# Second block's attention in a fused two-block kernel: hand-shakes by block, another order of normalising, the output projection's first two tiles together, and four of eight key copies behind the index loop

## What is computed

```python
q_lat = einsum('bshn,hnc->bshc', q_nope, w_uk)             # 8 sparse heads; the kernel turns w_uk onto the keys instead
logits = einsum('bqhd,bsd->bhqs', q_idx, k_idx)             # the index: 8 index heads
index  = einsum('bhqs,bqh->bqs', relu(logits), w_idx)       # masked causally
sel    = top_k(index, 128)                                  # keys that a query keeps
p      = softmax((q_lat . c_kv + q_rope . k_rope) * scale over sel)      # per sparse head
o_a    = (p @ c_kv) @ w_uv                                  # 8 sparse heads, 64 wide
o_b    = dilated_attention(q_b, k_b, v_b)                   # 8 dilated heads, 64 wide, a bias table in place of masks
x      = x + concat(o_a, o_b) @ w_out                       # layer "out2"
```

## Time and profile before

| | us |
|---|---|
| median of three runs (lowest, highest) | 1631.54 (1627.67, 1635.12) |
| the profiled execution | 1633.2 |
| its span | 1631.4 |
| TensorE busy | 1590.2 (97%) |
| VectorE, ScalarE, GpSimd busy | 877.9, 730.2, 599.9 |
| mean granted TensorE clock | 0.994 |

### The profile page before, as it was taken

One profiled execution on the slowest core, in us unless ns is written; L12 is line 12 of the kernel. 1 busy time (PEld: TensorE's weight loads), 2 busy tenths in 40 slices (PEclk: granted clock), 3 DMA queues, 4 the chain that ended last, 5 costly groups with the idle time before them and its releaser, 6 DMA issues.

```text
span 1631.4 us, 20643 instructions
## 1 busy us (share of the span) xinstructions
PE 1590.2 (97%) x7742; PEld 1296.7 (79%) x7742; DVE 877.9 (54%) x1117; ACT 730.2 (45%) x871; POOL 599.9 (37%) x254
## 2 busy tenths in 40 slices
PE   9999999999999899999999999889999999999997
PEld 7898887688887788888898687557878888888886
DVE  6254111781565799989875698442533642232314
ACT  5355132344244688887863422774243322221221
POOL 1421454043442133222225555554323344344441
PEclk9999999999999999999999999999999999999998
DMA  5321243222225999999964336002411222232221
GB/s 199 123 72 52 78 142 116 78 78 103 81 105 200 393 421 405 389 393 392 389 247 143 103 104 169 29 1 78 155 52 52 104 90 93 101 103 90 92 102 52
DMA packets 49617, 251.52 MB, mean 154 GB/s; under 512 B 9936, under 2 KB 12752, under 8 KB 23312
## 3 DMA queue, kind: packets, MB, share of 16 engines
q1 hardware_dynamic: 43200, 237.85, 40.0%
q0 software_dynamic: 5184, 8.40, 1.4%
q10 hardware_dynamic: 1168, 4.39, 0.7%
HBM read 235.00 MB, written 16.78 MB: 154 GB/s over the span
## 4 chain that ended last, share of the span: by engine, by line
PE 74%; issue 12%; DVE 6%; POOL 3%; ACT 2%; DMA 2%; PEld 0%; SPq 0%; ACTq 0%; DVEq 0%; POOLq 0%; PEldq 0%
PE psum L232 21%; PE psum L234 21%; PE psum L233 21%; POOL w_lo L148 3%; DVE kept_bias L2173 1%; PE psum L2320 1%; DVE top L2172 1%; PE psum L2355 1%; PE psum L2343 1%; PE psum L2600 1%; DMA moe_w<-in_w_moe 1%; PE psum L1310 1%; PE psum L710 1%; ACT w_hi L142 1%; PE psum L729 1%
## 5 line engine op out<-in xcount | busy, mean ns | idle before, releaser
L148 POOL TENSOR_TENSOR w_lo<-raw,w_hi 128x2048 fp32r<-128x2048 f32 x91 | 418.9, 4604 | 666.5 <-ACT w_hi L142 631.6
L142 ACT ACTIVATE w_hi<-raw 128x2048 fp32r<-128x2048 f32 x95 | 181.5, 1911 | 326.9 <-PE psum L234 326.8
L232 PE MATMUL psum<-x_hi,w_hi 128*128 128x512 f32 (+1 forms) x816 | 316.3, 388 | 2.4 <-ACT k_sparse L2108 1.7
L233 PE MATMUL psum<-x_lo,w_hi 128*128 128x512 f32 (+1 forms) x816 | 314.1, 385 | 0.0
L234 PE MATMUL psum<-x_hi,w_lo 128*128 128x512 f32 (+1 forms) x816 | 314.1, 385 | 0.0
L1328 DVE TENSOR_TENSOR moe_lo<-moe_w,moe_hi 128x2048 fp32r<-128x2048 f32 x100 | 228.0, 2291 | 32.7 <-ACT moe_hi L1318 31.6
L1318 ACT ACTIVATE moe_hi<-moe_w 128x2048 fp32r<-128x2048 f32 x100 | 191.2, 1915 | 28.5 <-PE psum L234 16.9
L232 PEld LDWEIGHTS psum<-x_hi,w_hi 128*128 128x128 f32 x816 | 153.3, 188 | 34.7 <-ACT k_sparse L2108 2.5
L233 PEld LDWEIGHTS psum<-x_lo,w_hi 128*128 128x128 f32 x816 | 153.3, 188 | 31.2 <-issue 0.7
L234 PEld LDWEIGHTS psum<-x_hi,w_lo 128*128 128x128 f32 x816 | 153.3, 188 | 30.7
L232 PE MATMUL psum<-y_hi,w_hi 128*128 128x512 f32 x352 | 138.0, 392 | 0.3 <-issue 0.3
(11 more groups left out here) (389 smaller groups left out, 2854.7 us busy)
## 6 DMA issues: line engine op xcount, KB each, us to landing
raw<-in_w_dense SPq DMA_DIRECT2D x95, 1024.0 KB, 4.8
moe_w<-in_w_moe_ahead SPq DMA_DIRECT2D x54, 1024.0 KB, 14.2
moe_w<-in_w_moe SPq DMA_DIRECT2D x48, 1024.0 KB, 14.9
yrow<-expert_rows SPq DMA_DIRECT2D x8, 512.0 KB, 7.2
res<-in_x SPq DMA_DIRECT2D x4, 512.0 KB, 6.6
decay<-in_decay SPq DMA_DIRECT2D x8, 256.0 KB, 5.1
hn_rows<-hn_tok ACTq DMA_DIRECT2D x4, 512.0 KB, 8.3
out<-res SPq DMA_DIRECT2D x4, 512.0 KB, 2.7
```

Of the source, the lines that this page charges most:

```text
L142: act.activation(w_hi[c % RING][:, :], raw[c % RING][:, :], ACT.Copy).then_inc(hi_ready, 1)
L148: pool.tensor_tensor(w_lo[c % RING][:, :], raw[c % RING][:, :], w_hi[c % RING][:, :].bitcast(F32), ALU.subtract).then_inc(lo_ready, 1)
L232: pe.matmul(out, lh, rh, start=first, stop=False, **more)
L233: pe.matmul(out, lh, rl, start=False, stop=False, **more)
```

## The change

1. *Index loop.* The latent keys are made after turns 3, 8, 13, 18, in banks 3, 0, 1, 2, each with its own wait for the bank. Only the first four copies stay in the loop (after turns 5, 7, 10, 12); the other four come behind it on ScalarE. q_rope waits for four copies, q_b for eight.
2. *Hand-shakes by block.* VectorE signals each of the three rest blocks, ScalarE waits for each, and TensorE signals the 384 block by itself (`s_mid`). The rest blocks get places of their own: 384 in bank 2, 256 and 128 in bank 3. S(1) waits for the v_b tiles bank by bank and not for all of them at once.
3. *Order on VectorE.* normalise(k+1) stands between softmax(k+2, 0) and softmax(k+2, 1).
4. *ScalarE's start.* The copies of the latent values are mixed with the exponentials of head 1, and the split of the second out2 chunk moves from before the head loop to its turn 4.
5. *out2.* Its first two tiles are built together, kt by kt, and the last T and V stand ahead of kt 2, 3 and 4.

```diff
-                for m in range(per):
+                if together and b == 0 and i == 0:
+                    steps = [(m, kt) for kt in range(kts) for m in range(per)]
+                else:
+                    steps = [(m, kt) for m in range(per) for kt in range(kts)]
+                for m, kt in steps:
...
-    LATENT_AT = (4, 9, 14, 19)
-    LATENT_READ_AT = tuple(u + i for u in LATENT_AT for i in (2, 3))
+    LATENT_AT = (3, 8, 13, 18)
+    LATENT_READ_AT = (5, 7, 10, 12)
+    LATENT_BANK = (3, 0, 1, 2)
...
+                latent_key(LATENT_READ_AT.index(u))
+        for h in range(HEADS // 2, HEADS):
+            latent_key(h)
         dense_act(act, "q_rope")
...
         def latent_keys(p):
-            pe.matmul(psum[:, p, :], w_uk[:, 2 * p:2 * p + 2, :].rearrange("p h c -> p (h c)"), c_kv[:, :],
+            pe.wait_ge(bank_free, FIRST_TILE["q_rope"] + p + 1)
+            pe.matmul(psum[:, LATENT_BANK[p], :], w_uk[:, 2 * p:2 * p + 2, :].rearrange("p h c -> p (h c)"), c_kv[:, :],
                       start=True, stop=True).then_inc(ql_done, 1)
...
-        pe.wait_ge(ql_read, HEADS)
         for name in ("q_rope", "q_b", "k_b"):
+            if name != "k_b":
+                pe.wait_ge(ql_read, HEADS // 2 if name == "q_rope" else HEADS)
             dense_pe(pe, name, x_hi, x_lo)
...
-    rest_z = flat[:, 1024:1024 + SPAN - S]
+    rest_z = {2: flat[:, 1024:1024 + 3 * P], 1: flat[:, 1536:1536 + 2 * P], 0: flat[:, 1792:1792 + P]}
...
-                    if h >= 2 and qt == TB - 2:
-                        pe.wait_ge(rest_read, COUNTED + h)
+                    out = rest_z[qt]
+                    if h >= 2 and qt:
+                        pe.wait_ge(rest_read, COUNTED + 3 * (h - 1) + (1 if qt == TB - 2 else 3))
+                if h == 1 and qt:
+                    pe.wait_ge(bank_free, FIRST_TILE["out2"] - 2 + 2 * (TB - 1 - qt))
+                if h == 2 and qt == TB - 1:
+                    pe.wait_ge(bank_free, FIRST_TILE["out2"] + 4)
...
-        pe.wait_ge(bank_free, FIRST_TILE["out2"] + 4)
...
-        dense_pe(pe, "out2", y_hi, y_lo, norm=Parts(av_low, COUNTED),
-                 step_hooks={4: lambda: [transposes(A_HEADS - 2), values(last - 1)],
-                             5: lambda: [transposes(A_HEADS - 1), values(last)]})
+        dense_pe(pe, "out2", y_hi, y_lo, norm=Parts(av_low, COUNTED), together=True,
+                 step_hooks={2: lambda: transposes(A_HEADS - 2),
+                             3: lambda: [values(last - 1), transposes(A_HEADS - 1)],
+                             4: lambda: values(last)})
...
         softmax(0, 1)
+        softmax(1, 0)
         normalise(0)
-        softmax(1, 0)
         softmax(1, 1)
         for k in range(A_HEADS + 2):
             if k + 2 < A_HEADS:
                 softmax(k + 2, 0)
-                softmax(k + 2, 1)
             if k + 1 < A_HEADS:
                 normalise(k + 1)
+            if k + 2 < A_HEADS:
+                softmax(k + 2, 1)
...
         weigh(act, 0, 1)
-        for q in range(TB):
-            values_of_latents(q)
+        weigh(act, 1, 0)
+        values_of_latents(0)
+        values_of_latents(1)
+        weigh(act, 1, 1)
+        values_of_latents(2)
+        values_of_latents(3)
...
-        split_hi(act, FIRST_CHUNK["out2"] + 1, FIRST_TILE["out2"])
         for k in range(A_HEADS + 2):
+            if k == 4:
+                split_hi(act, FIRST_CHUNK["out2"] + 1, FIRST_TILE["out2"])
```

More of the change, by code:

```diff
@@ L244, in dense_pe @@
     def dense_pe(pe, name, ah, al, n_tok=S, kts=KT, hooks=None,
-                 norm=None, tile_hooks=None, by_parts=False, step_hooks=None):
+                 norm=None, tile_hooks=None, by_parts=False, step_hooks=None, together=False):
         n, k = turns(name)
@@ L256, in body @@
                     pe.wait_ge(lo_ready, c0 + b + 1 + k * i)
-                for m in range(per):
+                if together and b == 0 and i == 0:
[3 more added lines that the diff above has]
+                for m, kt in steps:
                     j = per * b + m
                     bank = (t0 + j) % 4
[L260 to L270, removed]
+                    if kt == 0:
+                        pe.wait_ge(bank_free, t0 + j + 1 + k * per * i)
+                    if step_hooks and k * per * i + j == 0 and kt in step_hooks:
+                        step_hooks[kt]()
+                    if norm and j == 0 and not (by_parts and i):
+                        norm.wait_split(pe, kt + 1)
+                    mm = three_pass(pe, psum[:, bank, 0:n_tok], wh[:, m, kt, :], wl[:, m, kt, :],
+                                    ah[:, kt, 0:n_tok], al[:, kt, 0:n_tok], kt == 0, kt == kts - 1)
+                    if kt == kts - 1:
+                        mm.then_inc(tile_done, 1)
+                        if tile_hooks and k * per * i + j in tile_hooks:
+                            tile_hooks[k * per * i + j]()
                 if hooks and k * i + b in hooks:
@@ L2279, in build @@
     a_in = sem("att_in")
[L2280 removed]
+    va_done, va_read, s_done, wide_read, rest_read, s_mid, s_exp, s_inv, s_norm, s_norm_pool, t_done, t_read, \
         av_done, av_high, av_low = (
@@ L2386, in softmax @@
             scale = (HD + 32) ** -0.5 if h < HEADS else HD ** -0.5
-            lo, blocks, z, read = ((0, (3,), wide_z[h % 2] if h else first_wide, wide_read),
-                                   (S, (2, 1, 0), rest_z if h else first_rest, rest_read))[part]
+            read = (wide_read, rest_read)[part]
             if h >= 3 and part == 0:
@@ L2394, in softmax @@
                 dve.wait_ge(a_in, 144 + 32)
-            dve.wait_ge(s_done, COUNTED + 2 * h + part + 1)
-            for qt in blocks:
+            for qt in ((3,), (2, 1, 0))[part]:
                 n = P * (qt + 1)
                 o = SEG[n]
-                ins = dve.tensor_tensor_reduce(
-                    out=score_of(h)[:, o:o + n], in0=z[:, o - lo:o - lo + n],
-                    in1=(bias if h < HEADS else dil_bias)[:, o:o + n], scale=-scale, scalar=3e38,
-                    op0=ALU.add, op1=ALU.min, accum_out=snmax[b][:, qt:qt + 1])
-            ins.then_inc(read, 1)
+                if h and qt == TB - 2:
+                    dve.wait_ge(s_mid, COUNTED + h)
+                else:
+                    dve.wait_ge(s_done, COUNTED + 2 * h + part + 1)
+                if h == 0:
+                    z = first_rest[:, o - S:o - S + n] if part else first_wide
+                else:
+                    z = rest_z[qt] if part else wide_z[h % 2]
+                dve.tensor_tensor_reduce(
+                    out=score_of(h)[:, o:o + n], in0=z, in1=(bias if h < HEADS else dil_bias)[:, o:o + n],
+                    scale=-scale, scalar=3e38, op0=ALU.add, op1=ALU.min,
+                    accum_out=snmax[b][:, qt:qt + 1]).then_inc(read, 1)
         def normalise(h):
@@ L2427, in weigh @@
         b = h % 3
-        act.wait_ge((wide_read, rest_read)[part], COUNTED + h + 1)
         for qt in ((3,), (2, 1, 0))[part]:
             n = P * (qt + 1)
+            if part:
+                act.wait_ge(rest_read, COUNTED + 3 * h + TB - 1 - qt)
+            else:
+                act.wait_ge(wide_read, COUNTED + h + 1)
             ins = act.activation(score_of(h)[:, SEG[n]:SEG[n] + n], score_of(h)[:, SEG[n]:SEG[n] + n], ACT.Exp,
```

23 lines of the change are left out of this document (8 added, 15 removed).

## The result

| | before | changed |
|---|---|---|
| median (lowest, highest), runs | 1631.47 (1627.67, 1635.12), 4 | 1621.67 (1620.58, 1622.61), 4 |
| ratio, 95% interval | | 0.994 [0.9916, 0.9963] |
| profiled execution, span | 1633.2, 1631.4 | 1622.61, 1620.8 |

What follows compares the result with a forecast made beforehand. TensorE was taken as the bound, so gains are its waits or earlier releases. Terms 0.8 + 0.9 + 2.6 + 2.3 + 3.1 + 0.9 = 10.6 us, clock effects cancelling, took 1631.54 to 1620.9, range 1618 to 1624.

Steps and rivals of the forecast that it cites:

- The bound: Whole kernel: TensorE holds 74% of the chain, so gains must be its waits or moments that release it.
- A: Index loop's copies and latent matmuls: q_rope starts earlier, most is given back at v_b's third piece; 0.8 us gained.
- B: Start of the head loop: S(1) waits for v_b's tiles bank by bank; 0.9 us gained (0.5 to 1.0).
- C: S(1) to T(2): T(1)'s wait goes, 0.7 of T(2)'s 1.32 stays; 2.6 us gained (1.3 to 3.3).
- D: T(2) to T(6), sparse heads: TensorE becomes the bound, 0.6 wait left at T(6); 2.3 us gained (1.0 to 2.9).
- E: T(6) to T(12), three dilated pairs: each goes from 9.82 to 8.78 us; 3.1 us gained (0 to 5.1).
- The ring: Head loop's cycle of engine waits per head pair: 9.82 us before, 8.78 with the reciprocal 1.04 earlier.
- ScalarE becomes the ring: Rival for the head loop, chance 0.13: ScalarE's waits don't shrink, only 5.2 us gained, time 1626.3.
- slower: Rival, chance 0.04: the parked softmax part 1 delays TensorE in the head loop; 2.8 us slower, 1634.3.
- F: out2's first two tiles together: matmuls cover V(7)'s wait for ScalarE; 0.9 us gained (0.3 to 1.5).
- The clock: Head loop's low-clock stretch goes, 1.6 us back; a new one at v_b's third piece costs 1.7; they cancel.
- no low stretch at v_b: Rival, chance 0.24: the idle stretch before v_b's third piece leaves the clock up; 12.2 us gained, time 1619.3.

Runs made afterwards that it cites:

- x1: The kernel before with the index loop's edits alone; 1633.09 us, ratio 1.0005.
- x2: The changed kernel with the index loop's edits undone; 1620.53 us, ratio 0.9924.
- x7: The changed kernel with ScalarE's start undone: latent values' copies ahead of head 1's exponentials, weight split before the head loop; 1623.42 us, ratio 0.9933.
- x5: The changed kernel with VectorE's order alone undone, normalise(k+1) again behind both softmax parts; 1628.88 us, ratio 0.9966.
- x4: The kernel before with VectorE's new order alone, normalise(k+1) between the softmax parts; 1624.95 us, ratio 0.9958.
- x8: The changed kernel with k_b's last rotary product two top-k rounds earlier and, for even dilated heads, normalising ahead of both softmax parts; 1613.7 us, ratio 0.9877.
- x6: The changed kernel with out2's first two tiles built one after the other again; 1622.56 us, ratio 0.9925.
- x3: The changed kernel with the last rotary product of k_b two of VectorE's top-k rounds earlier; 1616.93 us, ratio 0.9900.

## Why the prediction held, step by step

**The bound.** Right: the waits that were taken from TensorE behind v_b came off the time, and the rest of the program (482.8 to 483.4) gave nothing back. ("1.21 to 1.99 us before every even head's T" is a slip: 1.99 is T(1)'s, an odd head's; the even ones waited 1.21 to 1.69.)

**A, index loop: 0.8 forecast, 0.98 measured** (78.39 to 77.41 from the first index matmul to v_b3, in the changed kernel and in x1 alike). The mechanism was right: VectorE, not TensorE, set the third piece, and TensorE's lead was given back as one idle stretch. Two sizes were wrong. "q_rope starts near 935.2", a lead of 3.9, followed the waits for ReLU and sum and left out TensorE's own work, 15.05 us in the loop: the lead could be 17.95 - 15.05 = 2.9 at most, and is 2.68. The idle stretch is then 2.68 - 0.98 + 0.31 = 2.01 (0.31 is what x2 shows without the lead) and not the 3 to 4 that was given as a sign. And the 0.82 that VectorE could gain "at most" is 1.00: at the first stall I took the usual 0.10 off the printed 0.44, but the row that opens a query block otherwise starts 0.08 before its neighbour's end (933.47 + 0.62 to 934.01 in before), so 0.52 was lost there.

**B, S(1) bank by bank: 0.9, measured 0.98** (19.62 to 18.64 in x2, which has no low stretch and a wait of 0.31 at the third piece like before). No run undoes it alone. S(1) starts 0.23 behind the last matmul of v_b (1020.69 to 1020.92).

**C, S(1) to T(2): 2.6, measured 3.28** (18.01 to 14.73). T(1)'s wait is gone, as said. At T(2) I left 0.7 and 0.33 stayed; the last 0.30 is TensorE's busy time for the same matmuls, 14.71 before and 14.41 after. x7 ties the term to ScalarE's part, the cause that was named; x5 shows that 0.83 of it needs VectorE's order too.

**D, sparse heads: 2.3, measured 2.88.** Of the waits of 2.90, 0.39 stayed at T(6), where I had left 0.6, and TensorE's busy time fell from 17.91 to 17.53. x7 prices the split in turn 4 at 0.14: without it ScalarE is busy for 14.83 of the 17.79 us, which leaves room for its 1.90.

**E, dilated pairs: 3.1, measured 3.09** (31.04 - 26.35 = 4.69, less the 1.6 of before's low stretch). The ring came out as 8.79 against 8.78, member by member. x4 and x5 show the cause from both sides: the order. The parked softmax part 1 stayed hidden, so neither "ScalarE becomes the ring" nor "slower" came about; x8 shows in addition that VectorE may wait 1.62 at a reciprocal without harm.

**F, out2: 0.9, measured 1.07**; x6 gives 1.08. The 0.6 that was held against it is there (out2's first matmul waits 0.90 and not 0.29), but it comes with the order: x4 and x6 have it as well. In x4 the waits of the step are 1.80 in place of 1.60 (0.41 before T(14) is gone), and the step is as long as before (59.21, 59.18).

**The clock: both halves as forecast.** No low stretch in the changed head loop (1.6 back), one at v_b (1.63 lost, by x2). The rival "no low stretch at v_b" would have had a step to S(1) of 18.6, and it is 20.27.

**The sum.** The terms without the clock are 0.98 + 0.98 + 3.28 + 2.88 + 3.09 + 1.07 = 12.3, and I had 10.6; C and D make up 1.3 of the difference, A, B and F 0.4. With the clock (1.6 - 1.63) and 0.5 in the last step it is 12.7 from the first index matmul to the end (710.29 to 697.56). That the spans differ by 10.6, the very sum of the forecast, is chance: the untouched stages ahead of the loop ended 2.13 later in this execution. So the forecast of the median (1620.9 against 1621.67) is closer than its terms were, and part of that is luck. What stays open is where between 9.8 (the medians) and 12.7 (the steps) the mean gain lies; the interval of the ratio, 6.0 to 13.7 us, holds both. The later runs of before (medians 1633.61 and 1633.47, not beside the changed kernel's four) would make it 11.9.

## What to carry to other kernels

An engine that gets a lead must be able to use it: take its own work off first (here that capped the lead at 2.9), ask who frees the next buffer, and move that release by as much, or the lead becomes an idle stretch that costs the clock on top (x1: nothing; x3: 3.9 us). In a ring of engines look for work that stands ahead of the ring's member only by the order of the program; moving it behind is worth its full length in each round until TensorE's own work is the bound, here 1.04 and then another 0.77 a pair. Where untouched stages scatter by microseconds, compare steps between landmarks, which here repeat within 0.05.

## What the runs showed of the hardware

Every one of the five traces with an idle stretch of 2.0 in front of v_b's third piece (changed, x1, x5, x6, x7) has the 1.2 GHz level right behind it, with a granted clock of 0.60 to 0.68 over the 2.4 to 3.6 us that follow, and it costs 1.63 (changed against x2) to 1.65 (x1 against before) in the step to S(1). None of the five with at most 0.31 there (before, x2, x3, x4, x8) has it; x3 and x8 keep the loop's edits and lack only the wait. (x5, x6 and x7 reach the place within 0.6 us of each other, so the five are not five independent cases.) I had argued by an idle stretch of 3.4, near the 4 at the earlier trace rows; 2.0 was enough. Elsewhere a wait of that size is followed by it at some times and not at others: the wait before T(1), 1.99 in before (no fall) and 1.98 in x1 (0.71 over 1034 to 1038); 1.7 at q_rope, without a fall in before and with one in x4; and within x5 the three waits of 1.99, with, without and with. So the length of the wait alone doesn't decide. The Trainium skill ("TensorE: Matmul & The Clock Gate", Part 1) says of the clock's rise that its point differs between runs of one kernel; that is not shown here, but these traces show the like for the fall.

What a low stretch costs depends on whether TensorE has a wait behind it that takes it in: 1.6 in T(6) to T(12) of before and of x5, and 0.20 at T(1) of x1. What makes the place at v_b so regular wasn't tried: the 2.01 there follows 60 us of nearly unbroken work, and the traces don't say whether that matters.
